# Moving the low-half subtraction of 324 weight pieces from GpSimd into VectorE's program

## The reference, cut to what matters

```python
h = modulate(rms_norm(x, norm1_w[l]), sh1, sc1)
mix = hybrid_mixer(h, w_in[l], ...)            # h @ w_in, 8 heads of chunked delta rule
x = x + g1[:, None, :] * mix
h = modulate(rms_norm(x, norm2_w[l]), sh2, sc2)
x = x + g2[:, None, :] * swiglu(h, w_ffn_in[l], w_ffn_out[l])
# then, in the second block: gla_mixer, swiglu_2, mla_mixer, swiglu_2

def swiglu(h, w_ffn_in, w_ffn_out):
    gu = h @ w_ffn_in
    return (jax.nn.silu(gu[..., :D_FF]) * gu[..., D_FF:]) @ w_ffn_out
```

## Time and profile before

| | us |
|---|---|
| median of 3 runs | 1662.66 |
| runs | 1652.23, 1662.66, 1664.63 |
| profiled execution, time | 1662.97 |
| profiled execution, span on the core | 1661.3 |

### The profile page before, as it was taken

How to read it: one execution, slowest core, us unless ns; L and a number is a source line. 1 busy time by engine, 2 the same in 40 slices (tenths; PEclk the granted TensorE clock), 3 DMA queues, 4 the chain that set the end, 5 groups by cost and what they waited for, 6 DMA issues and landing times.

```text
span 1661.3 us, 29299 instructions
## 1 busy us (share of the span) xinstructions
PE 1521.5 (92%) x10457; PEld 1320.7 (80%) x10457; DVE 692.2 (42%) x1198; ACT 648.9 (39%) x1171; POOL 726.0 (44%) x400
## 2 busy tenths in 40 slices
PE   5999999999998989998988787989999799899997
PEld 3987778877786768887876776779999577799997
DVE  2555445655432243342234444354532122345522
ACT  3543444444322043333345333155553322255542
POOL 4544344333200046565644331058888000178884
PEclk8899999999998989999998877889999888999998
DMA  8566553556244959996762323056657016056563
GB/s 290 169 207 190 177 175 103 189 177 194 74 137 154 317 180 260 264 275 208 236 182 72 93 76 94 20 153 183 182 164 222 28 54 179 13 166 185 169 177 100
DMA packets 399982, 269.44 MB, mean 162 GB/s; under 512 B 9914, under 2 KB 357424, under 8 KB 399936
## 3 DMA queue, kind: packets, MB, share of 16 engines
q1 hardware_dynamic: 399936, 268.83, 54.6%
HBM read 267.75 MB, written 1.05 MB: 162 GB/s over the span
## 4 chain that ended last, share of the span: by engine, by line
PE 43%; issue 33%; POOL 15%; DVE 5%; ACT 3%; DMA 0%; POOLq 0%; DVEq 0%; ACTq 0%; SPq 0%
POOL w_low L612 14%; PE bank L711 10%; PE bank L712 9%; PE bank L713 9%; PE bank L752 4%; PE bank L1048 1%; PE bank L662 1%; PE bank L996 1%; PE bank L1080 1%; DVE scratch L1980 1%; PE bank L1108 1%; PE bank L1107 1%; PE bank L1088 1%; DVE scratch L1978 1%; PE bank L650 1%
## 5 line engine op out<-in xcount | busy, mean ns | idle before, releaser
L612 POOL TENSOR_TENSOR w_low<-w_raw,w_high 128x1024 fp32r<-128x1024 f32 (+2 forms) x324 | 712.4, 2210 | 913.0 <-ACT w_high L1191 913.0
L711 PE MATMUL bank<-h_parts,w_high 128*128 128x256 f32 x1824 | 555.2, 304 | 26.7 <-DVE h_parts L1637 24.5
L712 PE MATMUL bank<-h_parts,w_high 128*128 128x256 f32 x1824 | 525.6, 288 | 0.0
L713 PE MATMUL bank<-h_parts,w_low 128*128 128x256 f32 x1824 | 524.8, 288 | 0.0
L711 PEld LDWEIGHTS bank<-h_parts,w_high 128*128 128x128 f32 x1824 | 358.6, 197 | 60.8 <-issue 47.9
L712 PEld LDWEIGHTS bank<-h_parts,w_high 128*128 128x128 f32 x1824 | 360.6, 198 | 4.2 <-issue 3.9
L713 PEld LDWEIGHTS bank<-h_parts,w_low 128*128 128x128 f32 x1824 | 359.4, 197 | 0.0
L1191 ACT ACTIVATE w_high<-w_raw 128x1024 fp32r<-128x1024 f32 (+2 forms) x324 | 312.7, 973 | 54.3 <-DMA w_raw<-in_ffn_w_out 22.6
L1918 DVE TENSOR_TENSOR act_parts<-evac,act_parts 128x256 f32 x66 | 138.5, 2098 | 55.0 <-ACT act_parts L1401 55.0
L1183 ACT ACTIVATE evac<-bank 128x256 f32<-128x256 f32 x140 | 53.9, 385 | 264.1 <-PE bank L713 221.3
L711 PE MATMUL bank<-act_parts,w_high 128*128 128x256 f32 x528 | 150.8, 286 | 0.0
(11 more groups left out here) (335 smaller groups left out, 1843.5 us busy)
## 6 DMA issues: line engine op xcount, KB each, us to landing
w_raw<-in_ffn_w_in SPq DMA_DIRECT2D x88, 512.0 KB, 3.8
w_raw<-in_w_in SPq DMA_DIRECT2D x72, 512.0 KB, 3.7
ada_w<-in_ada_w SPq DMA_DIRECT2D x34, 1024.0 KB, 5.3
w_raw<-in_w_ffn_in SPq DMA_DIRECT2D x44, 512.0 KB, 6.4
ada_w<-in_w_ada SPq DMA_DIRECT2D x16, 1024.0 KB, 10.0
w_raw<-in_gla_w_in SPq DMA_DIRECT2D x24, 512.0 KB, 3.7
w_raw<-in_ffn_w_out SPq DMA_DIRECT2D x32, 384.0 KB, 3.7
w_raw<-in_ffn_w_out SPq DMA_DIRECT2D x32, 320.0 KB, 3.3
```

Of the source, the lines that this page charges most:

```text
L612: pool.tensor_tensor(w_low[:, s, 0:n], w_raw[:, s, 0:n], w_high[:, s, 0:n].bitcast(F32), ALU.subtract)\
L711: pe.matmul(acc[:, 0:T], hi[:, n, :], x_parts[:, k, 0, :], start=k == 0, stop=False)
L712: pe.matmul(acc[:, 0:T], hi[:, n, :], x_parts[:, k, 1, :], start=False, stop=False)
L713: mm = pe.matmul(acc[:, 0:T], lo[:, n, :], x_parts[:, k, 0, :], start=False, stop=k == kb - 1)
```

## The change

The 324 subtractions leave GpSimd's program, which then ends after its setup. VectorE gets the same function `low` with the same semaphores, and its calls are spread over VectorE's program by hand, each at a point of the stage in which the piece is split. The loops whose last pass differs are unrolled by one pass, and the FFN output loop gets its own function `add_down`. In the first FFN's loop the call of `ada_copy` comes to stand after `low`. SP, ScalarE and TensorE are not edited.

```diff
@@ gpsimd @@
-            def low(st, i, j, parts):
-                n, s = len(parts[j % len(parts)]) * P, j % st.slots
-                pool.wait_ge(S("rounded"), st.piece(i, j))
-                pool.tensor_tensor(w_low[:, s, 0:n], w_raw[:, s, 0:n], w_high[:, s, 0:n].bitcast(F32), ALU.subtract)\
-                    .then_inc(S("split"), 1)
-            for st, parts in ((st_h1, IN_PARTS), ..., (st_d3, OUT_PARTS)):
-                with pool.Fori(0, st.n) as i:
-                    for j in range(st.per):
-                        low(st, i, j, parts)
@@ vector @@
+            def low(st, i, j, parts):
+                m, s = len(parts[j % len(parts)]) * P, j % st.slots
+                dve.wait_ge(S("rounded"), st.piece(i, j))
+                dve.tensor_tensor(w_low[:, s, 0:m], w_raw[:, s, 0:m], w_high[:, s, 0:m].bitcast(F32), ALU.subtract)\
+                   .then_inc(S("split"), 1)
...
             h_low(0, KB - 1, h1_parts)
+            for j in range(3):
+                low(st_h1, 0, j, IN_PARTS)
             dve.wait_ge(S("rows_landed"), 16 * n_table_dmas)
             dve.tensor_copy(pos_f[:, :], pos_i[:, :]).then_inc(S("pos"), 1)
+            for j in range(3, 6):
+                low(st_h1, 0, j, IN_PARTS)
...
+            for j in range(6, 9):
+                low(st_h1, 0, j, IN_PARTS)
             dve.wait_ge(S("padded"), 3)
             dve.wait_ge(S("c_ready"), 6)
             for k in range(TAPS1):
                 convolve(0, k)
...
+            low(st_h1, 1, 0, IN_PARTS)
             ada_copy(PRE - 1)
             short_conv(0)
             ada_bias(PRE - 1, 4 * PRE - 4)
+            low(st_h1, 1, 1, IN_PARTS)
@@ head1: low(i, 2) after the masks L1780, low(i, 3) after L1787, low(i, 4) after L1804 @@
                     if gemm:
                         if l == LEVELS - 1:
                             ada_copy(m - 1, spare=True)
+                        if l < LEVELS - 1:
+                            low(st_h1, i, l + 4, IN_PARTS)
+                        elif not last:
+                            low(st_h1, i + 1, 0, IN_PARTS)
...
                 if gemm:
                     short_conv(i)
                     ada_bias(m, 4 * PRE - 4 + 4 * i)
+                    if not last:
+                        low(st_h1, i + 1, 1, IN_PARTS)
@@ add_down, the FFN output loop @@
+                    for j in range(8):
+                        if step and j == 7:
+                            ada_copy(step[0] + i)
+                        if j % 4 == 3:
...
+                        if j < 5:
+                            low(st, i, j + 3, OUT_PARTS)
+                        elif not last:
+                            low(st, i + 1, j - 5, OUT_PARTS)
@@ ffn @@
             def ffn(n, st_f, st_d, step=None, step_out=None):
+                low(st_f, 0, 0, IN_PARTS)
                 norm_scale(n, *norm_cols(n))
...
                 h_low(n, KB - 1, h_parts)
+                for j in (1, 2):
+                    low(st_f, 0, j, IN_PARTS)
...
                     for q in range(2):
-                        if step and q:
-                            ada_copy(step[0] + i)
-
+                        if q == 0:
+                            low(st_f, i, 3, IN_PARTS)
+                        elif not last:
+                            low(st_f, i + 1, 1, IN_PARTS)
+                        else:
+                            low(st_d, 0, 1, OUT_PARTS)
                         prod = evac[:, 2 * q, :]
                         dve.wait_ge(S("evacuated"), st_f.done(i, 2 * q + 1) + 3)
                         dve.tensor_tensor(prod, prod, evac[:, 2 * q + 1, :], ALU.mult).then_inc(S("ffn_act"), 1)
+                        if not last:
+                            low(st_f, i + 1, 2 * q, IN_PARTS)
+                        else:
+                            low(st_d, 0, 2 * q, OUT_PARTS)
+                        if step and q:
+                            ada_copy(step[0] + i)
                         dve.wait_ge(S("act_high"), first + 2 * i + q + 1)
@@ before the GLA heads: low(0, 0) ahead of the norm; low(0, 1..3) after h_low; low(0, 4), then the gates' scan @@
             dve.wait_ge(S("gate_log"), 2)
+            low(st_h2, 0, 5, IN_PARTS)
+            for j in range(3):
+                low(st_h2, 1, j, IN_PARTS)
@@ head2 @@
                 dve.tensor_tensor(qe, q, cum, ALU.mult).then_inc(S("scaled2"), 1)
+                if gemm:
+                    low(st_h2, i, 3, IN_PARTS)
+                    low(st_h2, i, 4, IN_PARTS)
...
@@ low(i, 5) after the attention sums, low(i+1, 0) and low(i+1, 1) ahead of the wait for o2_rn @@
                 dve.tensor_tensor(r, r, on2, ALU.mult).then_inc(S("head2_out"), 1)
+                if gemm and not last:
+                    low(st_h2, i + 1, 2, IN_PARTS)
```

More of the change, by code:

```diff
@@ L1769, in _, with head1 @@
             ada_bias(PRE - 1, 4 * PRE - 4)
-            def head1(i, gemm, chain):
+            low(st_h1, 1, 1, IN_PARTS)
+            def head1(i, gemm, last=False):
                 n = i
@@ L1849, in head1 @@
                 dve.tensor_tensor(part(oall, c), part(oall, c), onrm, ALU.mult).then_inc(S("head_out"), 1)
-            with dve.Fori(1, H1) as i:
-                head1(i, True, True)
-            head1(H1, False, True)
+            with dve.Fori(1, H1 - 1) as i:
+                head1(i, True)
+            head1(H1 - 1, True, last=True)
+            head1(H1, False)
             dve.wait_ge(S("gates"), 2)
@@ L1874, in norm_cols, with add_blocks @@
                 return vec_cols[:, w_col:w_col + KB], sc_col
-            def add_blocks(st, per, sem, first, step=None, pieces=1):
+            def add_blocks(st, per, sem, first, step):
                 with dve.Fori(0, st.n) as i:
                     for j in range(per):
-                        if step and j == per // 2:
+                        if j == per // 2:
                             ada_copy(step[0] + i)
-                        dve.wait_ge(S("evacuated"), st.done(i, j * pieces + pieces - 1) + 3)
+                        dve.wait_ge(S("evacuated"), st.done(i, j) + 3)
                         xf = xT[:, bass.ds(per * i + j, 1), :]
@@ L1887, in add_blocks, with add_down, blocks @@
                         dve.tensor_tensor(sq[:, bass.ds(per * i + j, 1), :], xf, xf, ALU.mult).then_inc(S("norm_sq"), 1)
+                    ada_bias(step[0] + i, step[1] + i * step[2])
+            def add_down(st, first, step=None):
+                def blocks(i, last=False):
+                    for j in range(8):
+                        if step and j == 7:
+                            ada_copy(step[0] + i)
+                        if j % 4 == 3:
+                            b = j // 4
+                            dve.wait_ge(S("evacuated"), st.done(i, j) + 3)
+                            f = slice(2 * i + b, 2 * i + b + 1) if last else bass.ds(2 * i + b, 1)
+                            dve.tensor_tensor(xT[:, f, :], xT[:, f, :], evac[:, b, :], ALU.add).then_inc(S("d_added"), 1)
+                            dve.wait_ge(S("d_added"), first + 2 * i + b + 1)
+                            dve.tensor_tensor(sq[:, f, :], xT[:, f, :], xT[:, f, :], ALU.mult).then_inc(S("norm_sq"), 1)
+                        if j < 5:
+                            low(st, i, j + 3, OUT_PARTS)
+                        elif not last:
+                            low(st, i + 1, j - 5, OUT_PARTS)
                     if step:
                         ada_bias(step[0] + i, step[1] + i * step[2])
+                with dve.Fori(0, st.n - 1) as i:
+                    blocks(i)
+                blocks(st.n - 1, last=True)
             def add_pairs(st, first):
@@ L1922, in ffn @@
                         ada_bias(step[0] + i, step[1] + i * step[2])
-                add_blocks(st_d, 2, "d_added", 2 + FFN_OF[n] * KB, step_out, pieces=4)
+                with dve.Fori(0, st_f.n - 1) as i:
+                    hidden(i)
+                hidden(st_f.n - 1, last=True)
+                add_down(st_d, 2 + FFN_OF[n] * KB, step_out)
             add_blocks(st_o1, 4, "o_added", 4, (M_WO, 14 * KB - 4, 6 * KB))
             ffn(1, st_f1, st_d1, (M_FFN1, 8 * KB, 4), (M_D1, 14 * KB + 4 * (H1 - 1), 4))
+            low(st_h2, 0, 0, IN_PARTS)
             norm_scale(2, *norm_cols(2))
@@ L1934, in _ @@
             h_low(3, KB - 1, h1_parts)
+            for j in (1, 2, 3):
+                low(st_h2, 0, j, IN_PARTS)
             dve.memset(segment, 1.0).then_inc(S("segment"), 1)
@@ L2015, in head2 @@
                 dve.tensor_tensor(r, r, on2, ALU.mult).then_inc(S("head2_out"), 1)
-            with dve.Fori(1, H2) as i:
+                if gemm and not last:
+                    low(st_h2, i + 1, 2, IN_PARTS)
+            with dve.Fori(1, H2 - 1) as i:
                 head2(i)
-            head2(H2)
+            head2(H2 - 1, last=True)
+            head2(H2, gemm=False)
             add_pairs(st_o2, 4 + KB)
```

23 lines of the change are left out of this document (16 added, 7 removed).

## The result

| | before | changed |
|---|---|---|
| median of 20 runs, us | 1662.45 | 1666.01 |
| lowest to highest, us | 1642.96 to 1664.63 | 1660.21 to 1671.98 |
| profiled execution: span / time, us | 1661.3 / 1662.97 | 1663.6 / 1665.3 |

Changed against before: 1.0047, 95% interval 1.0027 to 1.0066. The kernel is half a per cent slower, less than the 1% that a measurement of this kernel can tell.

The account below looks back on a forecast made before the run. The prediction took TensorE to bound the kernel, busy 1521.5 of 1661.3 us and waiting more for VectorE than for the subtraction. Its sum: 1663.0 + 46 - 25 - 10 + 5 - 5 = 1674 us, range 1645 to 1697.

Parts of the forecast that it names:

- The price: One 128x1024 subtraction on VectorE: 1.22 us, 1.14 of VectorE's time, about 360 us over 324 pieces.
- Term 1: First FFN's input loop: the adaLN copy behind the subtraction stalls TensorE and lowers its clock in 11 passes, +46 us.
- the rival of the covered copy: First FFN: the adaLN copy's new place is covered, 1619 us; chance 0.13, shared with larger gains in the heads.
- The rival in which the gaps keep their clock: First FFN's input loop: the stalls don't lower TensorE's clock, so +29 us there and 1657 in all; chance 0.15.
- Term 2: GLA heads: VectorE multiplications no longer stretched beside GpSimd, TensorE's waits gone and clock higher, -25 us.
- Term 3: Three FFN starts: scale and h_parts no longer stretched, clock back sooner, -3.4 us each, -10 in all.
- Term 4: First stage: low(0, 0) behind all eight h_parts delays piece 0, and first head's q/k sums come later, +5 us.
- Term 5: First FFN's output: TensorE's 5.6 us wait for adaLN rows shrinks, -5 us.
- At nothing: First mixer's eight heads, the second and third FFN input loops and the two output loops: no change expected.
- the slower rival: First mixer: the adaLN load burst comes late, 3 us in 7 heads, +21 us, 1695 in all; chance 0.22.

Follow-up runs that it names:

- e1: Changed kernel with the first FFN's adaLN copy moved back ahead of the wait for piece 3: 1607.66 us, ratio 0.9682 to the kernel before.
- e5: Kernel before, subtraction still on GpSimd, with the first FFN's adaLN copy behind the product and the split of piece (i + 1, 2): 1709.55 us, ratio 1.0335.
- e3: Changed kernel plus seven unread matmuls on TensorE ahead of the adaLN sum in each of 11 first-FFN passes: 1638.55 us, ratio 0.9865 to the kernel before.
- e4: Kernel before with only the GLA heads' 24 subtractions moved to VectorE, the adaLN copy at its old place: 1625.1 us, ratio 0.9797.
- e7: Changed kernel, adaLN copy moved back ahead, plus 18 unneeded 128x1024 GpSimd subtractions in the GLA heads: 1631.47 us, ratio 0.9877 to the kernel before.
- e2: Changed kernel with the first FFN's adaLN copy between the product and low(i + 1, 2): 1633.12 us, ratio 0.9840 to the kernel before.
- e6: Changed kernel, adaLN copy moved back ahead, some first-stage and GLA-head subtractions moved to other places on VectorE: 1597.44 us, ratio 0.9664 to the kernel before.

## Why the prediction was right, and where not

The forecast of 1674 lies 8 us above the median, and the stretch from 1646 to 1679.3 that holds the result had the largest chance, 0.51. By its own terms:

**The price, 1.22 us.** Right: 1.23 alone, 2.35 for two in a row, so 1.14 to the next start. 324 of them are 360.1 us, as worked out.

**Term 1, +46.** Measured +45.9, and each part is shown. Stall: 3.28 us against 3.5 in each pass, 35.5 us in all where 38.5 stood (e1 takes it away with one line, e5 makes it on the old kernel). Clock: 1.5 per pass, 16.5 in all, was taken from single gaps; 20.1 us of the loop in e3 are 1.8 per pass. That the term is right to 0.1 us is luck in so far as these two errors cancel. The bias wait of 9.4 us went as forecast and for the reason given: VectorE has a whole piece for it, from 665.89 to TensorE's 670.13, and in e5, with GpSimd still at work, the bias is ready 4.9 us before TensorE comes for it. What the prediction did not have is a second reason, which is enough by itself: without GpSimd the act_parts subtraction ahead of the bias takes 0.42 us instead of 2.27, and e1 is free of the wait with the copy at its old place. The loop is 9.9 us faster than before in e1, which is the rival of the covered copy made real: 1607.66, where 1619 was worked out with the same 9 us in it. The rule of the Trainium skill (TensorE: Matmul & The Clock Gate, HAM oscillation) agrees with this trace: a wait in every pass held the loop's clock at 0.88, at a price of 20.1 us. The rival in which the gaps keep their clock (1657) falls by e3.

**Term 2, -25.** Too small. The heads gave 29.8 and their start 4.4. The mechanism stands (e4 has it alone, e7 takes it back with GpSimd's work alone), the terms were mis-sized in three places. TensorE's idle time in the heads went from 30.7 to 20.5 us (below), -10.2 where -12.7 stood: the 15.1 us of waits at L996 are gone and the kt/qt products take 0.28 us throughout (24 of them below, mean ns). The wait at L975, the old L988, grew from 8.4 to 9.6 us where 2.3 were priced. But low(i, 5), put at nothing behind the attention sums, holds up the states, 3.8 us at L994. The other 19.6 us are busy time, from 142.3 to 122.7, at a mean granted clock of 0.95 instead of 0.83. The prediction had 11.4, from the attention matmuls alone. And the norms with the first piece of the GLA stage were a fourth start of the kind of term 3, of which only the 1.2 us at piece 5 had been counted.

```profile
L2041 DVE TENSOR_TENSOR scratch<-scratch 128x128 f32<-128x128 f32 x24 | 6.8, 283 | 0.0
```

The heads in the trace of before and after, the same matmuls:

```profile
915.00:1088.00 173.00, 142.34 (x803) 127.20 (x801) 78.11 (x200) 52.72 (x77) 37.16 (x17) 0.83 0.27 74
```

```profile
956.50:1099.70 143.20, 122.71 (x803) 110.88 (x802) 74.69 (x219) 52.70 (x77) 0.00 (x0) 0.95 0.32 86
```

**Term 3, -10.** It gave 5.7: 2.2, 2.6 and 0.9 where 3.4 each stood. At the second FFN:

```profile
1103.67 0.55 PE L698 MATMUL bank<-h_parts,w_high 128*128 128x256 f32 x1 [2.77 <-DVE h_parts L1631]
...
1110.56 0.38 PE L698 MATMUL bank<-h_parts,w_high 128*128 128x256 f32 x1 [0.51 <-DVE w_low L1615]
...
1108.00:1115.00 7.00, 6.27 (x46) 5.66 (x47) 5.11 (x7) 5.40 (x9) 0.00 (x0) 1.00 0.44 127
```

The first wait for h_parts is 2.77 instead of 3.20, and the later gap of 2.00 us beside the stretched h_parts is gone; that part is worth 1.8 us at each of the three, as forecast. The clock is back at 1.00 in piece 1, but what it gives over the 0.5 us wait for w_low is 0.7 us by the lag, not 1.1, and nothing at the first start. The third gave 2.2 us up to 1455 and lost 1.5 again just behind, at a mean clock of 0.50 from 1455 to 1462 where the trace of before has 0.71 from 1454 to 1461.

**Term 4, +5.** The trace has +10.3, and 4.2 of it are not the change. TensorE's adaLN rounds ahead of it, alike in both programs, ran at the lower clock from 24 us on: the scale of VectorE starts at 40.05 instead of 35.81, and in the eight experiments at 33.5 to 40.0. Of those with the changed kernel's program up to there, e1 and e2 have 39.9, e7 36.8 and e3 33.5, so this is scatter between executions; e5, with the program of before, has 38.7. What remains is 6.1, by the mechanism as told:

```profile
40.05 0.17 DVE L1622 SCALAR_TENSOR_TENSOR nscale<-mod,n_cols 128x8 f32<-128x8 f32 x1
...
46.79 0.48 DVE L1631 SCALAR_TENSOR_TENSOR h_parts<-hT,mod,h_parts 128x256 fp32r<-128x256 f32 x1 [0.18 <-ACT h_parts L1203]
47.20 3.49 DVE L1615 TENSOR_TENSOR w_low<-w_raw,w_high 128x1024 fp32r<-128x1024 f32 x3
...
48.67 0.55 PE L698 MATMUL bank<-h_parts,w_high 128*128 128x256 f32 x1 [8.85 <-DVE w_low L1615]
```

The first low() stands behind all eight h_parts and TensorE starts piece 0 only at 48.67; less the 4.2 that is 44.4, the number of the prediction. At the end of the piece the lag is 6.6, so 2.3 of the change where 2.4 stood; the q/k sums of the first head add 3.7 where 2.2 stood. In e6 this stage loses nothing, though the clock of the adaLN rounds is the low one there as well:

```profile
24.00:45.00 21.00, 15.93 (x68) 9.40 (x68) 10.68 (x22) 5.98 (x9) 0.00 (x0) 0.50 0.89 240
```

**Term 5, -5.** -3.4 in the changed kernel, and -0.2 in e1. The wait for the adaLN rows, 5.6 us before, is 1.2 in the changed kernel and 5.1 again in e1: it shrank only because TensorE itself came late. This gain belongs to term 1 and goes with it.

**At nothing.** Right for the heads of the first mixer (L830 waits 2.7 us, L843 had 4.0) and for the other loops: 127 of 127 us busy in the second FFN's. The burst of adaLN loads, the slower rival, did not show: no such wait stands among TensorE's.

**The sum.** The terms give 1663.0 + 45.9 - 34.2 - 5.7 + 6.1 - 3.4 = 1671.7. The rest is what no term had: -5.6 in the third attention, -4.6 in the first mixer and +4.2 at the adaLN rounds. The first goes with a granted clock that differs between the traces, from a cause that is not shown, the last is scatter; for the first mixer the cause is not shown. So the terms' errors (9 too little in the heads, 4 too much at the FFN starts, one or two more in terms 4 and 5) cancelled in part. That the total came so near is in part luck.

What stays open: why TensorE's clock falls in every third pass at an idle time of 1.5 us and in each at 3.3, and what decides it in the adaLN rounds. The prediction had ordered single gaps by their length (2.6 us kept the clock, 2.8 lost it); e2 lost it at 1.5, so the length of one gap alone doesn't decide. In e5 the clock takes 2.9 us of a pass at 4.7 us of idle time, in the changed kernel 2.2 at 3.3; no run separates the length of the gap from its place.

## What to carry to other kernels

Moving work between engines is two edits: who does it, and behind what the neighbours now stand. Here the first was worth 54 us (e1 against before, some 6 of it in the third attention, which no edit touched) and one line of the second cost 58. Put the small operation for which the busiest engine waits ahead of the large one that waits for its own input. A stall in each pass of a loop costs its length and the clock: here 3.3 us cost 5.1, and filling the gap with matmuls that nobody reads showed the difference. And look for a helper engine's price in its neighbour's stretched operations, not in the waits for the helper itself.

## What the runs showed of the hardware

- VectorE and GpSimd hold each other up. VectorE operations of 0.28 to 0.42 us took 2.3 to 2.5 beside a GpSimd subtraction, and GpSimd's own went from 2.40 to 3.33 us on average where VectorE was busy beside it (e7). The Trainium skill (SBUF — State Buffer, Who interferes with whom) says that the two share a pair of ports, that the sharing is "an exclusive lock", and that a VectorE instruction with two inputs in SBUF contends with a GpSimd instruction that reads SBUF; the trace agrees, as the stretched act_parts of the kernel before ends at 638.04 where GpSimd's piece ends at 637.76.
- TensorE's granted clock answers to gaps unevenly: with 1.5 us of idle time in each pass every third pass lost 1.5 us (e2), with 3.3 us all lost 1.7 to 2.9 (changed), with the gap filled none (e3, granted clock 1.00).
- The same 40 us of program at the start had VectorE's scale at 33.5 to 40.1 us in five executions (e3, e7, e2, e1, changed). The mean granted clock from 24 to 36 us was 0.80, 0.71 and, for the last three, 0.50.
